# Summing the squares of a norm on TensorE quarter by quarter instead of adding them on VectorE first

## The chip, the cores and the metric

One core of a Trainium2 chip. TensorE (PE) multiplies matrices into eight PSUM banks, VectorE (DVE) and ScalarE (ACT) work element by element, SyncE (SP) issues the loads; the engines run their own instruction streams and meet at semaphores. The metric is the device time of one execution of the whole program, in microseconds: the median of several runs.

## The reference

Two transformer blocks over 256 positions and 1024 channels in float32, one after the other. The first has two layers, each of a token mixer (attention, latent attention, two convolution branches) and a feed-forward part. What matters here is the norm with which each part begins, and the residual ahead of it:

```python
def rmsnorm(x, g):
    xf = x.astype(jnp.float32)
    y = xf * lax.rsqrt(jnp.mean(xf * xf, axis=-1, keepdims=True) + NORM_EPS)
    return (y * g.astype(jnp.float32)).astype(x.dtype)
...
def channel_mixing(x, shift, scale, g_pre, w_up, ffn_conv, w_down, g_post):
    h = rmsnorm(x, g_pre) * (1.0 + scale) + shift
    a, b = jnp.split(h @ w_up, 2, axis=-1)
    y = (jax.nn.silu(causal_dwconv(a, ffn_conv)) * b) @ w_down
    return rmsnorm(y, g_post)
```

and in the block `x = x + gate * token_mixing(...)`, then `x = x + gate * channel_mixing(...)`.

## The kernel before

The activations lie transposed: 1024 channels are 8 chunks of 128 partitions, each with the 256 positions as columns, so `x` is 128 x 2048 and a *quarter* is two chunks (128 x 512). The program is a list of stages: m0, f0, m1, f1 of the first block (m a mixer, f a feed-forward part), then 16 stages of the second. Weights come in tiles of 128 x 1024 through a ring of 11 landing places. Every float32 product is made of three: ScalarE casts a weight tile to a high part (`whi`, L460), VectorE subtracts to get the low part (`wlo`, L472), activations are split the same way, and `mm3` (L512 to L514) adds high x high, high x low and low x high. A tile can't be used before its `w_lo` signal. ScalarE and VectorE split a few tiles ahead of TensorE, at places that are written out in their programs.

A stage of the first block that isn't m0 begins before its norm is known ("early" stages: f0, m1, f1). `early_scalar` and `early_vector` scale and add the last stage's output into `x` quarter by quarter (L886, L888), and make `u`, which is `x` times the channel gains, without the norm's factor, which is the same for all channels of a position (high part L826, low part L896). `early_tensor` (L576) multiplies three pairs of weight tiles by `u`: its `step` 0 to 9 takes one chunk of `u` each, 6 groups of 3 matmuls while all three projections are in it, 12 matmuls in steps 0 and 1 and 6 in each of steps 8 and 9, as the third projection lags by two steps. Meanwhile ScalarE squares each quarter (L824, L830: `square`, 0 to 3). To sum over channels, which lie on partitions, TensorE multiplies by a matrix of ones in plain float32 (L601); that gives the sum in all 128 partitions of bank 7 (`MISC`). Before the change VectorE first adds the four quarters of squares into one (`squares_vector`, L867, three adds, called in `early_vector` between quarters 2 and 3 of `u`), and TensorE then sums the two chunks left after step 4 (`SUMS_AFTER`), and signals `sumsq`.

From `sumsq` on: ScalarE takes a logarithm and an exponential (L681, L683), VectorE the variance (L858) and Newton steps (L689 to L693), then for each of the eight chunks the normed value (L926), ScalarE its high part `h` (L847) and VectorE the low part (L931). The results of the early projections are read from their banks with the norm's factor (`lead_vector`, L614 and L615; `lead_scalar`, L623), between splits of the next tiles. In an f stage the next projections (j = 3, 4, 5, each a pair of tiles, multiplied by `h`) follow, then down-projection 0, j = 6 and 7, down-projection 1, and so on. Each j is drawn through taps (L1150, L1154), silu (L1122) and a product `up_read` (L1164), which frees the bank, and `inner` (L1127, L1168), which the down-projection reads. j = 7 uses the bank of j = 4. In m1 there follow the fourth `cf` projection (L1507, L1754), and projections `scu`, `qk` with convolution taps on VectorE (L1769).

Engines take their instructions strictly in this written order, waiting at each semaphore.

Of the kernel before, what the change touches and what calls it, by code (L numbers as in the profile page):

```python
# [11 lines left out]
ALU = mybir.AluOpType  # L12
# [4 lines left out]
T = 256  # L17
# [267 lines left out]
def lead_operand(g):  # L285
    return Lead(g.ra1[:, 2528:6656].rearrange("p (a n) -> p a n", a=2))


def bc2(ap):
    return ap.unsqueeze(1).broadcast_to([ap.shape[0], 2, ap.shape[1]])  # L290


def v2(ap):
    return ap.rearrange("p (a t) -> p a t", a=2)


def xk(t, k):
    return t[:, k * T:(k + 1) * T]
# [165 lines left out]
def split_vector(g, dve, upto):  # L464
    D_, W = g.m.done, g.m.when
    while g.ahead["dve"] < min(upto, len(g.split)):
        i = g.ahead["dve"]
        n = g.split[i]
        g.ahead["dve"] = i + 1
        w = g.weights(n)  # L470
        dve.wait_ge(*W("w_hi", n))
        dve.tensor_tensor(w.lo, g.slot(n), w.hi.bitcast(F32), ALU.subtract).then_inc(*D_("w_lo", n))  # L472
        modulation_vector(g, dve, n)
# [30 lines left out]
def take_tensor(g, pe, name, i):  # L504
    g.skip("pe")
    n = g.next("pe", name, i)
    pe.wait_ge(*g.m.when("w_lo", n))
    return n


def mm3(pe, out, w, x, first, last, skip=False):
    pe.matmul(out, w.hi, x.hi, start=first, stop=False, skip_group_check=skip)  # L512
    pe.matmul(out, w.hi, x.lo, start=False, stop=False, skip_group_check=skip)  # L513
    return pe.matmul(out, w.lo, x.hi, start=False, stop=last, skip_group_check=skip)  # L514
# [10 lines left out]
def halves(j):  # L525
    return 2 * j, 2 * j + 1
# [26 lines left out]


EARLY_STAGES = ("f0", "m1", "f1")
LEAD, LAG, SUMS_AFTER = 3, 2, 4
LEAD_ORDER = ((1, 0), (2, 0), (0, 0), (0, 1), (1, 1), (2, 1))


# [11 lines left out]
def lead_banks(st, j):  # L571

    return (j, 4 + j) if st[0] == "m" else (4 + j, j)


def early_tensor(g, pe, st, projections):  # L576


    D_, W = g.m.done, g.m.when
    u, parts, sums = lead_operand(g), [], g.ps[MISC]  # L580
    pe.wait_ge(*W("u_shift", st))
    for step in range(8 + LAG):
        if step < 8:
            pe.wait_ge(*W("u", st, step))
        for j, (name, at) in enumerate(projections):
            k = step - LAG * (j == LEAD - 1)
            for i, half in enumerate(halves(at)):
                bank = lead_banks(st, j)[i]
                if k == 0:
                    pe.wait_ge(*W(*g.banks.use(bank, "lead_read", st, 2 * j + i)))  # L590
                    parts.append(take_tensor(g, pe, name, half))
                if 0 <= k < 8:
                    mm = mm3(pe, g.ps[bank][:, 0:WIDE], g.weights(parts[2 * j + i])[:, k * 128:(k + 1) * 128], u.chunk(k),
                             k == 0, k == 7, skip=True)
                    if k == 7:
                        mm.then_inc(*D_("tile", parts[2 * j + i]))
        if step == SUMS_AFTER:
            pe.wait_ge(*W(*g.banks.use(MISC, "newton", st, 0)))
            pe.wait_ge(*W("squares", st, 3))
            for c in range(2):  # L600
                mm = pe.matmul(sums[:, 0:T], g.C("ones", 0, 128), xk(squares_buffer(g, st), c), start=c == 0, stop=c == 1)  # L601
            mm.then_inc(*D_("sumsq", st))


def lead_out(g, i):
# [38 lines left out]
MISC = 7  # L644
# [71 lines left out]
def quarter(p):  # L716
    return slice(p * 512, (p + 1) * 512)
# [48 lines left out]
def squares_buffer(g, st):  # L766
    return g.fa1[:, 2048:4096] if st in FIRST else g.fa2[:, 13056:15104]
# [90 lines left out]
    dve.tensor_scalar(g.small[:, 0:T], g.ps[MISC][:, 0:T], 1.0 / D, 1e-6, ALU.mult, ALU.add).then_inc(*D_("var", st))  # L858


def squares_vector(g, dve, st, p):
    D_, W = g.m.done, g.m.when
    sq = squares_buffer(g, st)
    dve.wait_ge(*W("square", st, p))
    if p > 1:
        dve.wait_ge(*W("squares", st, p - 1))
    dve.tensor_tensor(sq[:, quarter(0)], sq[:, quarter(0)], sq[:, quarter(p)], ALU.add).then_inc(*D_("squares", st, p))  # L867


def early_vector(g, dve, st, shift, A):  # L870

    D_, W = g.m.done, g.m.when
    u, prev = lead_operand(g), BEFORE[st]
    v, r = g.small[:, 0:T], g.small[:, T:2 * T]
    ysquare_vector(g, dve, prev)
    dve.wait_ge(*W("u_shift_hi", st))
    dve.tensor_tensor(u.shifts()[1], g.mod[:, shift:shift + 8].unsqueeze(2).broadcast_to([128, 8, 2]),
                      u.shifts()[0].bitcast(F32), ALU.subtract).then_inc(*D_("u_shift", st))
    split_vector(g, dve, g.ahead["dve"] + 1)
    normed_vector(g, dve, prev)  # L880
    dve.wait_ge(*W("gain", st))
    for p in range(5):
        if p < 4:
            t, s = g.t(p), g.x[:, quarter(p)]
            dve.wait_ge(*W("y_gated", prev, p))
            dve.tensor_tensor(v2(t), v2(t), bc2(r), ALU.mult).then_inc(*D_("y_scaled", prev, p))  # L886
            dve.wait_ge(*W("y_scaled", prev, p))
            dve.tensor_tensor(s, s, t, ALU.add).then_inc(*D_("x", st, p))  # L888
        if p == 4:
            squares_vector(g, dve, st, 1)  # L890
            squares_vector(g, dve, st, 2)
            squares_vector(g, dve, st, 3)
        for k in halves(p - 1) if p else ():
            c = u.chunk(k)
            dve.wait_ge(*W("u_hi", st, k))
            dve.scalar_tensor_tensor(c.lo[:, 0:T], xk(g.x, k), A[:, k:k + 1], c.hi[:, 0:T].bitcast(F32), ALU.mult,  # L896
                                     ALU.subtract).then_inc(*D_("u", st, k))
        if p == 1:
            split_vector(g, dve, g.ahead["dve"] + 1)
    split_vector(g, dve, g.ahead["dve"] + 2)  # L900


def modulated_vector(g, dve, st, gname, lay, shift, scale):
# [11 lines left out]
    if st != "m0":  # L915
        early_vector(g, dve, st, a - scale + shift, A)
        var_vector(g, dve, st)
# [53 lines left out]
def ysquare_vector(g, dve, st):  # L971

    D_, W = g.m.done, g.m.when
    sq = g.fa1[:, 2048:4096]
    for p in (1, 2):
        dve.wait_ge(*W("ysquare", st, p))
        if p == 2:
            dve.wait_ge(*W("ysquares", st, 1))
        dve.tensor_tensor(sq[:, quarter(0)], sq[:, quarter(0)], sq[:, quarter(p)], ALU.add).then_inc(*D_("ysquares", st, p))
# [36 lines left out]
def normed_vector(g, dve, st):  # L1016
    D_, W = g.m.done, g.m.when
    v, r = g.small[:, 0:T], g.small[:, T:2 * T]
    dve.wait_ge(*W("var_ln", "y", st))
    dve.tensor_scalar(v, g.ps[MISC][:, 0:T], 1.0 / D, 1e-6, ALU.mult, ALU.add).then_inc(*D_("var", "y", st))  # L1020
    rsqrt_vector(g, dve, ("y", st), r, v, g.t(8)[:, 0:T], g.t(8)[:, T:2 * T])
    dve.wait_ge(*W("factor", "y", st))
# [70 lines left out]
def ffn_tensor(g, pe, st, up, up0, down, dn0, R):  # L1093
    early_tensor(g, pe, st, [(up, up0 + j) for j in range(LEAD)])
    for p in range(NF // 2):
        for j in halves(p):
            if j >= LEAD:
                proj_tensor(g, pe, up, up0 + j, up_bank(j), ("up_read", st, j), g.h, chunks("h", st) if j == LEAD else None)
        for q in downs_behind(p):
            down_tensor(g, pe, st, down, dn0 + q, q, R[q % 3])  # L1100
# [182 lines left out]
def mix_tensor(g, pe, st, lay):  # L1283
# [5 lines left out]
    for step, i, bank in mix_banks(lay):  # L1289
        ps = g.ps[bank] if bank is not None else None  # L1290
        if (step, i, bank) == lead[0] and lay:
            early_tensor(g, pe, st, [mix_projection(st, lay, *s)[:2] for s in lead])
        elif (step, i, bank) == lead[0]:
            lead_tensor(g, pe, [mix_projection(st, lay, *s) for s in lead], g.h, chunks("h", st))
# [2535 lines left out]
```

## Time and profile before

| | us |
|---|---|
| median of 3 runs | 3313.85 |
| the runs | 3311.53 to 3317.24 |
| the profiled execution: time | 3317.55 |
| the profiled execution: span | 3315.8 |
| PE busy | 3170.8 (96%) |
| DVE busy | 2488.2 (75%) |
| ACT busy | 1779.0 (54%) |

The span runs from the first to the last instruction; the time has a little more around it. Rows of the trace give an instruction's start, its duration, engine, line, output and inputs, and in brackets how long the engine was idle before it and who ended the wait. Matmuls overlap: a row of 0.28 us begins 0.12 us after the one before. PEclk is TensorE's granted clock as a share of full speed.

### The profile page before, as it was taken

What the parts mean: (1) busy time and instruction counts of PE and PEld (TensorE: products, weight loads), DVE (VectorE), ACT (ScalarE), POOL (GpSimd) and SP (SyncE); (2) the same over time, 40 slices, a digit from 0 to 9 for tenths busy, and PEclk for the clock granted to TensorE, in tenths of its full rate; (3) what the DMA queues carried; (4) which work ended last, traced back from release to release, by engine and by line L of the source; (5) the groups of instructions that cost most, each with busy time, mean ns of one, the idle gap of its engine ahead of it and who ended that gap; (6) DMA issues with size and microseconds to landing.
All of it is one profiled execution on the core that took longest, in us unless ns stands there. A gap on an engine that the chain in (4) does not pass through costs nothing.

```text
span 3315.8 us, 64468 instructions
## 1 busy us (share of the span) xinstructions
PE 3170.8 (96%) x27118; PEld 3082.9 (93%) x27118; DVE 2488.2 (75%) x3822; ACT 1779.0 (54%) x2723; POOL 3.0 (0%) x6
## 2 busy tenths in 40 slices
PE   6899999989999999989999999999999999998999
PEld 6889999888999999879999989999979999987999
DVE  8888799987887766787676667667667667678766
ACT  4556554555564545665454546455456455456544
POOL 0000000000000000000000000000000000000000
PEclk8999999999999999999999999999999999999999
DMA  7456478444746555435555544555544555543453
GB/s 288 130 178 225 167 277 321 145 126 138 244 173 230 169 189 187 157 99 188 190 184 187 189 134 169 187 182 191 188 137 149 187 184 189 188 165 103 162 190 129
DMA packets 164353, 597.94 MB, mean 180 GB/s; under 512 B 18240, under 2 KB 18272, under 8 KB 163936
## 3 DMA queue, kind: packets, MB, share of 16 engines
q1 hardware_dynamic: 164064, 593.81, 53.3%
q8 instruction: 215, 3.52, 0.4%
q14 instruction: 74, 0.61, 0.1%
HBM read 592.69 MB, written 1.05 MB: 179 GB/s over the span
## 4 chain that ended last, share of the span: by engine, by line
PE 74%; DVE 16%; ACT 6%; issue 2%; DMA 1%; SPq 0%; DVEq 0%; ACTq 0%
PE ps L512 24%; PE ps L513 24%; PE ps L514 24%; DVE wlo L472 4%; ACT whi L460 2%; DVE fa L1769 1%; DVE land L658 1%; DVE fa L2663 0%; DMA land<-w_ada 0%; DMA land<-w_in 0%; DVE tmps L691 0%; DVE h L2017 0%; DVE tmps L689 0%; PE ps L2515 0%; DVE tmps L2372 0%
## 5 line engine op out<-in xcount | busy, mean ns | idle before, releaser
L512 PE MATMUL ps<-h,whi 128*128 128x256 f32 x5280 | 1489.9, 282 | 34.9 <-DVE h L931 13.9
L514 PE MATMUL ps<-h,wlo 128*128 128x256 f32 x5328 | 1491.6, 280 | 0.0
L513 PE MATMUL ps<-h,whi 128*128 128x256 f32 x5280 | 1478.5, 280 | 0.0
L472 DVE TENSOR_TENSOR wlo<-land,whi 128x1024 fp32r<-128x1024 f32 (+1 forms) x1026 | 1210.4, 1217 | 252.1 <-ACT whi L460 250.7
L460 ACT ACTIVATE whi<-land 128x1024 fp32r<-128x1024 f32 (+1 forms) x1026 | 1023.8, 1045 | 155.5 <-PE ps L514 129.2
L512 PEld LDWEIGHTS ps<-h,whi 128*128 128x128 f32 x5280 | 997.1, 189 | 44.0 <-issue 27.2
L514 PEld LDWEIGHTS ps<-h,wlo 128*128 128x128 f32 x5328 | 1005.7, 189 | 0.0
L513 PEld LDWEIGHTS ps<-h,whi 128*128 128x128 f32 x5280 | 997.3, 189 | 0.8
L513 PE MATMUL ps<-y,whi 128*128 128x256 f32 x1472 | 410.9, 279 | 0.0
L512 PE MATMUL ps<-y,whi 128*128 128x256 f32 x1472 | 410.9, 279 | 0.0
L514 PE MATMUL ps<-y,wlo 128*128 128x256 f32 x1472 | 410.9, 279 | 0.0
L2214 ACT ACTIVATE tmps<-tmps 128x256 f32<-128x256 f32 x176 | 74.1, 421 | 487.2 <-DVE tmps L2245 487.2
L512 PE MATMUL ps<-ra,whi 128*128 128x256 f32 (+2 forms) x1088 | 314.2, 289 | 10.3 <-DVE ra L1674 5.8
L513 PE MATMUL ps<-ra,whi 128*128 128x256 f32 (+2 forms) x1088 | 308.0, 283 | 0.0
L514 PE MATMUL ps<-ra,wlo 128*128 128x256 f32 (+2 forms) x1088 | 307.3, 282 | 0.0
L512 PEld LDWEIGHTS ps<-y,whi 128*128 128x128 f32 x1472 | 276.6, 188 | 0.0
L514 PEld LDWEIGHTS ps<-y,wlo 128*128 128x128 f32 x1472 | 276.6, 188 | 0.0
L513 PEld LDWEIGHTS ps<-y,whi 128*128 128x128 f32 x1472 | 276.6, 188 | 0.0
L512 PEld LDWEIGHTS ps<-ra,whi 128*128 128x128 f32 (+1 forms) x1088 | 207.1, 190 | 14.9 <-issue 8.5
L513 PEld LDWEIGHTS ps<-ra,whi 128*128 128x128 f32 (+1 forms) x1088 | 207.1, 190 | 0.6
L2245 DVE TENSOR_TENSOR tmps<-ps,small 128x512 f32<-128x512 f32 x176 | 121.5, 690 | 114.6 <-PE ps L514 114.4
L514 PEld LDWEIGHTS ps<-ra,wlo 128*128 128x128 f32 (+1 forms) x1088 | 207.0, 190 | 0.0
(470 smaller groups left out, 2904.1 us busy)
## 6 DMA issues: line engine op xcount, KB each, us to landing
land<-w_gu SPq DMA_DIRECT2D x352, 512.0 KB, 3.6
land<-w_dn SPq DMA_DIRECT2D x176, 512.0 KB, 3.5
land<-w_in SPq DMA_DIRECT2D x136, 512.0 KB, 3.5
land<-w_ada SPq DMA_DIRECT2D x96, 512.0 KB, 4.4
land<-w_up SPq DMA_DIRECT2D x88, 512.0 KB, 3.8
land<-hg_in SPq DMA_DIRECT2D x64, 512.0 KB, 3.5
land<-w_down SPq DMA_DIRECT2D x44, 512.0 KB, 4.1
land<-ple_gate SPq DMA_DIRECT2D x32, 512.0 KB, 3.5
```

Source lines behind the costliest of these rows:

```text
L460: act.activation(w.hi, g.slot(n), ACT.Copy).then_inc(*D_("w_hi", n))
L472: dve.tensor_tensor(w.lo, g.slot(n), w.hi.bitcast(F32), ALU.subtract).then_inc(*D_("w_lo", n))
L512: pe.matmul(out, w.hi, x.hi, start=first, stop=False, skip_group_check=skip)
L513: pe.matmul(out, w.hi, x.lo, start=False, stop=False, skip_group_check=skip)
L514: return pe.matmul(out, w.lo, x.hi, start=False, stop=last, skip_group_check=skip)
L658: dve.scalar_tensor_tensor(w, w, 1.0, g.crow[:, :], ALU.mult, ALU.mult, accum_out=g.mod[:, i:i + 1]).then_inc(*D_("ada", i))
L1769: dve.scalar_tensor_tensor(o, M.cu[:, j, n:n + 256], g.P("cf_conv", lay * 124 + 4 * n + j), o, ALU.mult, ALU.add).then_inc(*D_("conv", st, ...
L2214: act.activation(b[:, 0:T], a[:, 0:T], ACT.Silu).then_inc(*D_("silu", st, j))
L2245: dve.tensor_tensor(v2(a), v2(g.ps[4 + j % 3][:, :]), bc2(r), ALU.mult).then_inc(*D_("up_read", st, j))
```

## The change

The constant `SUMS_AFTER` becomes a tuple of four steps. After step 2 TensorE waits for the bank and for the squares of quarter 0 and multiplies the two chunks of that quarter by the ones; after steps 4, 5 and 6 it does the same for quarters 1, 2 and 3, all accumulating into the same bank; `sumsq` is signalled with the last. VectorE's three adds and the function that made them are gone. It holds for f0, m1 and f1.

```diff
-LEAD, LAG, SUMS_AFTER = 3, 2, 4
+LEAD, LAG, SUMS_AFTER = 3, 2, (2, 4, 5, 6)
...
-        if step == SUMS_AFTER:
-            pe.wait_ge(*W(*g.banks.use(MISC, "newton", st, 0)))
-            pe.wait_ge(*W("squares", st, 3))
-            for c in range(2):
-                mm = pe.matmul(sums[:, 0:T], g.C("ones", 0, 128), xk(squares_buffer(g, st), c), start=c == 0, stop=c == 1)
-            mm.then_inc(*D_("sumsq", st))
+        if step in SUMS_AFTER:
+            p = SUMS_AFTER.index(step)
+            if p == 0:
+                pe.wait_ge(*W(*g.banks.use(MISC, "newton", st, 0)))
+            pe.wait_ge(*W("square", st, p))
+            for k in halves(p):
+                mm = pe.matmul(sums[:, 0:T], g.C("ones", 0, 128), xk(squares_buffer(g, st), k), start=k == 0, stop=k == 7)
+            if p == 3:
+                mm.then_inc(*D_("sumsq", st))
...
-def squares_vector(g, dve, st, p):
-    D_, W = g.m.done, g.m.when
-    sq = squares_buffer(g, st)
-    dve.wait_ge(*W("square", st, p))
-    if p > 1:
-        dve.wait_ge(*W("squares", st, p - 1))
-    dve.tensor_tensor(sq[:, quarter(0)], sq[:, quarter(0)], sq[:, quarter(p)], ALU.add).then_inc(*D_("squares", st, p))
...
-        if p == 4:
-            squares_vector(g, dve, st, 1)
-            squares_vector(g, dve, st, 2)
-            squares_vector(g, dve, st, 3)
```

## Rows read from the trace of the kernel before

**Rows 1.** The page: busy time by engine, and shares of the last chain.
```profile
PE 3170.8 (96%) x27118; PEld 3082.9 (93%) x27118; DVE 2488.2 (75%) x3822; ACT 1779.0 (54%) x2723; POOL 3.0 (0%) x6
...
PE 74%; DVE 16%; ACT 6%; issue 2%; DMA 1%; SPq 0%; DVEq 0%; ACTq 0%
```

**Rows 2.** Line L601: count, duration in ns (min/median/max), first and last start.
```profile
L601 PE MATMUL ps<-fa,con x12: 377/378/379, 404.7 to 961.8; 128*128 128x256 f32 x12
```

**Rows 3.** Timeline of PE in f0: start, duration (us), line, output and inputs.
```profile
404.62 0.28 PE L514 MATMUL ps<-ra,wlo 128*128 128x258 f32 x1
404.73 1.02 PE L601 MATMUL ps<-fa,con 128*128 128x256 f32 x4
...
405.71 0.28 PE L513 MATMUL ps<-ra,whi 128*128 128x258 f32 x1
...
413.50 0.28 PE L512 MATMUL ps<-h,fr 128*128 128x256 f32 x1
...
430.36 0.28 PE L512 MATMUL ps<-ra,whi 128*128 128x256 f32 x1
...
441.56 0.28 PE L512 MATMUL ps<-h,whi 128*128 128x256 f32 x1
```

**Rows 4.** Timeline of DVE in f0.
```profile
400.55 2.27 DVE L867 TENSOR_TENSOR fa<-fa 128x512 f32<-128x512 f32 x3
402.74 0.88 DVE L896 SCALAR_TENSOR_TENSOR ra<-x,small,ra 128x256 fp32r<-128x256 f32 x2
...
406.30 0.42 DVE L858 TENSOR_SCALAR small<-ps 128x256 f32<-128x256 f32 x1 [0.42 <-ACT tmps L681]
...
409.20 0.48 DVE L931 SCALAR_TENSOR_TENSOR h<-fa,mod,h 128x256 fp32r<-128x256 f32 x1 [0.18 <-ACT h L847]
...
414.62 0.48 DVE L931 SCALAR_TENSOR_TENSOR h<-fa,mod,h 128x256 fp32r<-128x256 f32 x1 [0.18 <-ACT h L847]
...
415.57 2.36 DVE L472 TENSOR_TENSOR wlo<-land,whi 128x1024 fp32r<-128x1024 f32 x2
...
429.13 0.43 DVE L1168 TENSOR_TENSOR ra<-tmps,ra 128x256 fp32r<-128x256 f32 x1 [0.49 <-ACT ra L1127]
...
440.65 0.41 DVE L1164 TENSOR_TENSOR tmps<-fa,ps 128x256 f32<-128x256 f32 x1
```

**Rows 5.** Timeline of ACT in f0.
```profile
399.86 0.63 ACT L824 ACTIVATE fa<-x 128x512 f32<-128x512 f32 x1 [0.69 <-DVE x L888]
...
405.80 0.48 ACT L681 ACTIVATE tmps<-ps,con 128x256 f32<-128x256 f32 x1 [2.59 <-PE ps L601]
...
414.50 3.89 ACT L460 ACTIVATE whi<-land 128x1024 fp32r<-128x1024 f32 x4
```

**Rows 6.** Timelines of DVE and PE in m1.
```profile
620.35 0.76 DVE L1754 SCALAR_TENSOR_TENSOR fa<-tmps,fa 128x256 f32<-128x256 f32 x2 [2.25 <-ACT tmps L1507]
...
629.95 2.35 DVE L472 TENSOR_TENSOR wlo<-land,whi 128x1024 fp32r<-128x1024 f32 x2
...
631.22 0.58 PE L512 MATMUL ps<-h,whi 128*128 128x256 f32 x1 [4.44 <-DVE wlo L472]
```

**Rows 7.** Timelines of DVE and PE in f1, at projection j=7.
```profile
998.25 0.41 DVE L1164 TENSOR_TENSOR tmps<-fa,ps 128x256 f32<-128x256 f32 x1
...
998.81 0.36 PE L512 MATMUL ps<-h,whi 128*128 128x256 f32 x1 [0.64 <-DVE tmps L1164]
```

**Rows 8.** Windows: stretch, length, busy PE PEld DVE ACT POOL, PEclk, DMA share, GB/s.
```profile
685.40:697.60 12.20, 5.91 (x30) 3.82 (x30) 10.44 (x33) 7.67 (x21) 0.00 (x0) 0.71 0.14 44
918.70:932.00 13.30, 11.14 (x94) 11.17 (x95) 10.95 (x17) 7.04 (x11) 0.00 (x0) 1.00 0.43 146
631.20:635.90 4.70, 4.68 (x22) 4.68 (x23) 4.70 (x11) 0.00 (x0) 0.00 (x0) 0.50 0.00 0
697.60:704.20 6.60, 6.34 (x23) 5.32 (x24) 5.49 (x20) 3.58 (x16) 0.00 (x0) 0.50 0.01 4
2455.20:2458.70 3.50, 3.37 (x16) 2.53 (x16) 0.00 (x0) 1.68 (x4) 0.00 (x0) 0.51 0.00 0
```

## The prediction

> **What bounds the kernel now.** I read the page first: TensorE is busy for 96% of the span and holds 74% of the chain that ended last, VectorE 16% [rows 1]. These are averages over 20 stages. The change touches three places only, the norms at the start of f0, m1 and f1, so I went there: the timelines of PE, DVE and ACT, one engine at a time, over the start of f0 (395 to 455 us), m1 (590 to 690) and f1 (950 to 1010), looking for who arrives last at each hand-over.
>
> In f0 TensorE works off `early_tensor` without a hole: steps 5 to 9 are 66 matmuls, and from the second of them at 405.71 to the first matmul on `h` at 413.50 there are 65 intervals, 0.120 us each [rows 3]. The sums at 404.73 wait for nobody: the three VectorE adds began at 400.55 and were over before 402.8 (2.27 us together), 1.9 us before TensorE came to them [rows 3, 4]. From the sums hangs a second chain: ScalarE stood idle for 2.59 us until they were done at 405.80 [rows 5], then VectorE takes the variance at 406.30, the Newton steps, eight chunks of `h` (the first done at 409.68, the last at 415.10) and the split of the next weight tile at 415.57 [rows 4]. So in `early_tensor` two chains run side by side: TensorE's own stream, and sums, factor, `h`, splits, taps on ScalarE and VectorE. The question for every edit is which of the two it lengthens, and how much the second has in hand.
>
> Its slack is small. In f0 TensorE reaches down-projection 0 at 430.36 while its last operand is done at 429.56 (0.80 us in hand), and projection j=7 at 441.56 while `up_read` of j=4, which frees its bank, ends at 441.06 (0.50 in hand) [rows 3, 4]. In f1 the same place is already late: TensorE idles 0.64 us for L1164 (998.25 + 0.41 = 998.66, resumed 0.15 later: I take 0.15 as the hand-over) [rows 7]. In m1 TensorE idles 4.44 us until 631.22 for the split that starts at 629.95, and the VectorE chain before it had waited last, 2.25 us until 620.35, for a ScalarE tanh which itself reads what the chain delivers [rows 6]. So in m1 and f1 the second chain sets the time, and in f0 it nearly does.
>
> **Removed: nine VectorE adds.** `squares_vector` runs three times in each stage; the three adds of f0 are one row, which holds 402.74 - 400.55 = 2.19 us of VectorE's stream [rows 4]; m1 and f1 have the same. What stands behind them is the low part of chunks 6 and 7 (L896, 402.74), which TensorE needs at step 6, after 407, and two splits; then VectorE waits for the variance, which needs the sums. All of it comes 2.19 us earlier and ends in a longer wait. Worth: 0.
>
> **Added: six f32 matmuls a stage.** The 12 records of L601 in three stages are two for each of the two matmuls [rows 2]. From the matmul at 404.62 to the second one behind the sums at 405.71 are 1.09 us, where two plain intervals would be 0.24: the pair costs 0.85 us [rows 3]. After the change there are four pairs instead of one: 3 x 0.85 = 2.55 us a stage on TensorE, 7.7 in all. That is a measured price of the same matmul in the same place; an end below it would need TensorE to have been waiting there, and it was not.
>
> **Moved: the last pair.** Before, all is summed after step 4. Now the pairs stand after steps 2, 4, 5 and 6, and `sumsq`, on which the whole second chain waits, is only signalled by the last. Ahead of it TensorE now has three more pairs (2.55) and steps 5 and 6 (2 x 18 matmuls x 0.120 = 4.31): 6.86 us later. The squares are no reason for it: ScalarE's last square starts at 399.86 and takes 0.63 [rows 5], long before step 5. The waits on `square` therefore cost nothing; behind each on PE's queue stand only the following steps.
>
> **What the later sums do, f0.** Everything of the second chain moves by 6.86, since it had waited for the sums (ACT idle 2.59). TensorE's own stream ends 2.55 later, at 416.05. (a) The first `h` comes at 409.68 + 6.86 + 0.15 = 416.7, 0.6 us idle; the last at 422.1, so projection j=3 ends about 422.8; three projections take 430.36 - 413.50 = 16.9, one 5.6, so the stream alone would end it at 421.7. (b) j=4 needs its split: ScalarE casts four tiles only after `h` (L460 at 414.50) [rows 5], VectorE's first split ends near 416.75, so 423.8: 0.9 idle. (c) j=4 and j=5 are 11.2 us, to 435.0; down-projection 0 needs the operand of 429.56, now 436.57: 1.6 idle, 6.21 behind before. (d) j=7 would start at 447.8 and gets its bank at 441.06 + 6.86 + 0.15 = 448.1: 6.5 behind. After that the trace shows TensorE without holes to the end of f0, so nothing absorbs it. The idle pieces are not further terms; together with the 2.55 they make up the 6.5.
>
> **m1.** The wait at 631.22 ends with a VectorE split of the second chain: 6.86 later. TensorE's 2.55 vanish in its wait, which grows from 4.44 to about 8.8 us. **f1.** The wait at 998.81 likewise: 6.86. Sum: 6.5 + 6.86 + 6.86 = 20.2 us. The profiled execution has a span of 3315.8 and a time of 3317.55, so 3336.0 and 3337.8 for it; it lies 3.7 above the median of the runs shown, 3313.85. I put the sum on the median: 3334.1.
>
> **The unknown: the clock.** The longer hole in m1 may change what the clock does. At the hole of 4.44 the granted clock was 0.50 of full speed from 631.20 to 635.90, 4.7 us that did 2.35 us of full-speed work. After other holes the half-speed stretch (1.2 GHz for 2.4) lasted from 3.5 us (0.51 from 2455.20) to 6.6 us (0.50 from 697.60 to 704.20) [rows 8]. So m1 may turn out 0.6 better or 1.0 worse than the sum; I take no change. In f0 and f1 new holes of 0.3 to 1.6 us appear where there were none or 0.64. Nearest rows: in the 13.3 us from 918.70, of which TensorE idled 2.16 in one hole at the start, the clock stayed 1.00; in the 12.2 us from 685.40 it was busy for 5.91 only, in pieces, and the clock fell to a mean of 0.71 [rows 8]. I take "stays"; the other end is up to 3.3 us in either stage (half of 6.6), part of which the 1.6 us hole would hide.
>
> The skill speaks against the change in two places. The Trainium skill, Perfetto Trace Analysis, section Matmul Optimizations, says that the matmul engine scales its power with utilisation, so matmuls should run back to back in batches; holes in three more batches would by that rule give the last rival below, and the trace so far bears it out only for long or clustered holes. Its section Identifying the Most-Contended Engine tells to optimise the engine with the highest occupancy first; this change puts work on it. Counted by that engine's work alone the sum would be that of the first rival, 7.7 us.
>
> **Rivals.**
> (1) *Only TensorE's own work counts*, the later chain being hidden: 3 x 2.55 = 7.7, 3321.5. For it: TensorE is the 96% engine. Against: the waits at 631.22 and 998.81, and 0.50 us of slack in f0. Chance 0.07.
> (2) *VectorE's relief comes through, faster.* If TensorE reached the sums before the adds were done, taking them away would bring `sumsq`, `h` and the splits forward by up to 2.19 a stage, and in m1 and f1 VectorE does pace TensorE. Price -3 x 2.19 = -6.6: 3307.3. It decides only if step 4 ends before about 402.8; it ends at 404.73, and the last pair moves later on top of that. Chance 0.03.
> (3) *Mostly hidden, no measurable change.* The change does not do what it says, or later parts absorb it: for instance ScalarE or VectorE regain the delay within the idle time that they have at other points of m1, down to 5 us or less. Against: the waits named are ends of this very chain. Chance 0.04, about 3317.
> (4) *The clock falls in f0 and f1 too*, and stays down longer in m1: 2 x 2 to 3.3, + 1: 3339 to 3342. Chance 0.13.
> The forecast has the remaining 0.73, with a range of its own from 3331 to 3337 (0.6 to 1.0 of the clock, 0.3 a stage on the hand-overs, some 1.5 of run to run spread).
>
> **Range.** 3326 to 3341: it takes in the forecast, most of (4) and the half-hidden cases between (1) and it, and leaves out (2), (3) and (1). What a measurement of this kernel can tell from no change is about 0.2%, 6.6 us. Faster by more than that 0.03, within it 0.04, slower 0.93.
>
> **What would show it.** L601 with 48 records instead of 12, L867 gone; PE's step 2 to step 9 longer by 2.55 us in each stage, with the last pair some 6.9 us later counted from the first matmul of the stage; ACT's idle time ahead of L681 about 9.5 us instead of 2.59; VectorE idle some 9 us before L858. In m1 the wait ahead of the split grows to 8 or 9 us, in f1 the wait at j=7 gives way to several (for `h`, for a split, for down-projection 0), in f0 the same ones appear. If the L601 rows come where I say but down-projection 0 in f0 is under 4 us late, the slack was misread; if m1 is right and f0 and f1 are off by 2 or more each, it is the clock; if the extra pairs cost other than 0.85, the price of interleaved f32 matmuls is wrong.

## The result: 0.66% slower, and the profile after

| | before | after |
|---|---|---|
| median, us | 3314.55 (4 runs) | 3337.11 (4 runs, 3336.49 to 3337.27) |
| ratio | | 1.0066, 95% interval 1.0054 to 1.0078 |
| profiled execution: time, span | 3317.55, 3315.8 | 3336.49, 3334.7 |
| f0, m1, f1 in the profiled execution | 195.77, 360.68, 189.24 | 202.65, 368.22, 194.93 |

A stage is measured here and below from its first matmul on `u` (the first of 258 columns) to that of the next such stage, and f1 to the first matmul on the squares of its output. The changed kernel is slower by 22.6 us on the medians and by 18.9 in the two profiled spans; 3334.1 had been forecast, 20.2 more. By stage the profiled pair gives +6.88, +7.54 and +5.69 where 6.5, 6.86 and 6.86 had been worked out. Behind f1, where both kernels have the same instructions, the changed one was 1.1 us shorter in this pair.

The page after, its busy times and the line of the sums (count, duration in ns, first and last start), answers [rows 1, 2]:

```profile
PE 3179.9 (95%) x27154; PEld 3090.4 (93%) x27154; DVE 2482.8 (74%) x3813; ACT 1776.0 (53%) x2723; POOL 3.0 (0%) x6
...
L603 PE MATMUL ps<-fa,con x48: 377/378/382, 400.3 to 983.1; 128*128 128x256 f32 x48
```

VectorE has nine instructions fewer and TensorE 36 more, and TensorE's share fell although it has more to do: what grew is its waiting. The timeline of PE in f0 after, answering [rows 3]:

```profile
400.33 1.03 PE L603 MATMUL ps<-fa,con 128*128 128x256 f32 x4
...
405.50 1.02 PE L603 MATMUL ps<-fa,con 128*128 128x256 f32 x4
...
408.51 1.03 PE L603 MATMUL ps<-fa,con 128*128 128x256 f32 x4
...
416.75 0.36 PE L512 MATMUL ps<-h,fr 128*128 128x256 f32 x1 [0.59 <-DVE h L921]
...
423.66 0.38 PE L512 MATMUL ps<-h,whi 128*128 128x256 f32 x1 [0.67 <-DVE wlo L472]
...
436.63 0.35 PE L512 MATMUL ps<-ra,whi 128*128 128x256 f32 x1 [1.51 <-DVE ra L1158]
...
448.00 0.36 PE L512 MATMUL ps<-h,whi 128*128 128x256 f32 x1
```

The four pairs are there (the fourth starts at 411.54), none waits for its squares, and behind them stand the holes in the order of the working: for the first `h`, for a split, for the operand of down-projection 0. The other two engines in f0 after, answering [rows 4, 5]:

```profile
402.18 2.36 DVE L472 TENSOR_TENSOR wlo<-land,fr 128x1024 fp32r<-128x1024 f32 x2 [0.47 <-ACT fr L460]
413.11 0.42 DVE L861 TENSOR_SCALAR small<-ps 128x256 f32<-128x256 f32 x1 [8.57 <-ACT tmps L684]
...
435.92 0.43 DVE L1158 TENSOR_TENSOR ra<-tmps,ra 128x256 fp32r<-128x256 f32 x1 [0.48 <-ACT ra L1117]
```
```profile
412.60 0.48 ACT L684 ACTIVATE tmps<-ps,con 128x256 f32<-128x256 f32 x1 [9.51 <-PE ps L603]
```

Before, the same splits were

```profile
403.53 2.35 DVE L472 TENSOR_TENSOR wlo<-land,fr 128x1024 fp32r<-128x1024 f32 x2
```

So VectorE reaches them 1.35 us earlier, not 2.19, as it now waits for ScalarE's casts (0.47 us here), and then it idles 8.57 us instead of 0.42 for the norm's factor. The freed time went into waits, whole. The operand of down-projection 0 ends at 436.35 where it was 429.56, with the stage starting 0.10 sooner: 6.9 us later. In m1 and f1 after, answering [rows 6, 7]:

```profile
644.91 0.58 PE L512 MATMUL ps<-h,whi 128*128 128x256 f32 x1 [7.13 <-DVE wlo L472]
...
1007.48 0.36 PE L512 MATMUL ps<-ra,whi 128*128 128x256 f32 x1 [1.48 <-DVE ra L1158]
...
1020.02 0.36 PE L512 MATMUL ps<-h,whi 128*128 128x256 f32 x1 [1.10 <-DVE tmps L1154]
```

In m1 the one long wait grew from 4.44 to 7.13 us. The stage had begun at 590.72 before and at 597.50 after, so the matmul behind that wait comes 644.91 - 631.22 - 6.78 = 6.91 us later within its stage. In f1 the matmul of j=7 comes 1020.02 - 998.81 - (965.73 - 951.40) = 6.88 later.

### The profile page after: what moved, and what is told of

It is laid out like the page before. It is cut to its first block, busy times and chain, and to the rows that moved or that the text cites. A ratio compares the mean times of both kernels' runs of the same rounds, so it can differ in the third digit from the quotient of the medians.

```text
span 3334.7 us, 64525 instructions
## 1 busy us (share of the span) xinstructions
PE 3179.9 (95%) x27154; PEld 3090.4 (93%) x27154; DVE 2482.8 (74%) x3813; ACT 1776.0 (53%) x2723; POOL 3.0 (0%) x6
## 4 chain that ended last, share of the span: by engine, by line
PE 74%; DVE 17%; ACT 6%; issue 3%; DMA 1%; SPq 0%; ACTq 0%; DVEq 0%
PE ps L512 24%; PE ps L513 24%; PE ps L514 24%; DVE wlo L472 4%; ACT whi L460 2%; DVE fa L1759 1%; DVE land L661 1%; DVE fa L2653 0%; DMA land<-w_ada 0%; DMA land<-w_in 0%; DVE tmps L694 0%; DVE tmps L692 0%; DVE h L2007 0%; PE ps L603 0%; DVE attn L2653 0%
## 5 line engine op out<-in xcount | busy, mean ns | idle before, releaser
L512 PE MATMUL ps<-h,whi 128*128 128x256 f32 x5280 | 1491.2, 282 | 38.7 <-DVE h L921 13.2
```

## The experiments

Stage lengths from the profiled execution of each kernel, in us, and the time against the kernel before, run on the same chip:

| kernel | f0 | m1 | f1 | ratio, 95% interval |
|---|---|---|---|---|
| before | 195.77 | 360.68 | 189.24 | |
| before, again | 195.61 | 361.51 | 188.05 | one run |
| changed | 202.65 | 368.22 | 194.93 | 1.0066 (1.0054 to 1.0078) |
| changed, again | 202.24 | 368.23 | 194.93 | one run |
| pe_load | 198.29 | 361.45 | 189.75 | 1.0017 (1.0008 to 1.0027) |
| late_signal | 199.51 | 364.72 | 193.35 | 1.0039 (1.0025 to 1.0053) |
| early_quarters | 197.73 | 363.35 | 191.28 | 1.0021 (1.0012 to 1.0031) |
| adds_kept | 202.83 | 367.71 | 195.92 | 1.0069 (1.0054 to 1.0084) |
| hole_filled | 202.37 | 367.30 | 194.90 | 1.0059 (1.0042 to 1.0076) |
| m1_only_early | 195.60 | 358.23 | 189.21 | 0.9999 (0.999 to 1.0008) |

Matmuls came in two paces at the same granted clock, which has to be known to read this table. The windows from 1040 to 1120 of five executions (before, before again, changed, changed again, adds_kept), all in f1 and dense, PE alone (busy time, matmuls, PEclk, DMA share, GB/s):

```profile
1040.00:1120.00 80.00, 80.00 (x682) 1.00 0.63 214
```
```profile
1040.00:1120.00 80.00, 80.00 (x688) 1.00 0.63 217
```
```profile
1040.00:1120.00 80.00, 80.00 (x687) 1.00 0.66 226
```
```profile
1040.00:1120.00 80.00, 80.00 (x688) 1.00 0.65 228
```
```profile
1040.00:1120.00 80.00, 80.00 (x682) 1.00 0.66 225
```

682 or 687 to 688 matmuls in the same 80 us. The kernel before had either (189.24 and 188.05 us of f1), so the pace is of the execution and not of the change. Shorter stretches of the slow pace stand in f0 and m1 as well. late_signal, early_quarters and m1_only_early have the slow one (0.1177 us a matmul), pe_load and hole_filled the fast one (0.1167). Like with like, the change costs f1 194.93 - 188.05 = 6.88 at the fast pace, and 195.92 - 189.24 = 6.68 at the slow one (with adds_kept).

**TensorE's added work without the later signal.** The kernel before with

```diff
             mm.then_inc(*D_("sumsq", st))
+        if step in (5, 6, 7):
+            if step == 5:
+                pe.wait_ge(*W("y_gated", BEFORE[st], 3))
+            for c in range(2):
+                pe.matmul(g.ps[3][:, 0:T], g.C("ones", 0, 128), xk(squares_buffer(g, st), c), start=c == 0, stop=c == 1)
```

> The kernel before (VectorE adds, one pair of sums after step 4), and three more pairs of the same f32 matmuls on TensorE after steps 5, 6 and 7, into a bank that nothing reads (they compute nothing that is used): TensorE's added work alone, with the signal of the sums where it was. Theory of two chains: TensorE's stream is 2.55 us longer a stage; that counts in f0 in full, vanishes in m1 in the 4.44 us wait, and counts less the wait of 0.64 in f1: 2.55 + 0 + 1.9 = 4.5 us over before. Rival, only TensorE's work counts: 7.7 us. If the matmuls are the whole cause of the 22 us: about 22.

Measured: 3321.64 against 3315.79, 5.9 us; by stage +2.5 in f0, -0.1 in m1 against the second trace of before (both have a half-speed stretch at 920 us, see below), +1.7 in f1 at the same pace. Expected were 2.55, 0 and 1.9; the stages add up to 4.2 us against 4.5. The interval of the time is 2.7 to 9.0 us, which leaves out 22 but not the 7.7 of the first rival; what speaks against that one is m1, which didn't grow. TensorE's work counts where it is the bound, and m1 swallows it. These pairs stand behind the signal of the sums. The same count of f32 matmuls as in the changed kernel, a quarter of its loss.

**The later signal without added work.**

```diff
-LEAD, LAG, SUMS_AFTER = 3, 2, 4
+LEAD, LAG, SUMS_AFTER = 3, 2, 6
```

> The kernel before with its single pair of sums after step 6 instead of step 4, nothing else: the signal comes two steps later (4.31 us), TensorE's work is the same. Two chains: 4.31 in m1 and f1, 3.8 in f0, where 0.5 is in hand: 12.4 us over before. Rival, only TensorE's work counts: 0.

Measured: 3328.98 against 3315.79, 13.2 us; by stage +3.74, +4.04, +4.11. Not one instruction was added. ScalarE's wait for the sums in f0, [rows 5] before, is now

```profile
409.98 0.48 ACT L681 ACTIVATE tmps<-ps,con 128x256 f32<-128x256 f32 x1 [6.94 <-PE ps L601]
```

2.59 + 4.35. The position of one pair of matmuls in TensorE's stream costs more than three pairs behind the signal do.

**All four pairs, as early as the single one.** The changed kernel with

```diff
-LEAD, LAG, SUMS_AFTER = 3, 2, (2, 4, 5, 6)
+LEAD, LAG, SUMS_AFTER = 3, 2, (1, 2, 3, 4)
```

> The changed kernel with its four pairs after steps 1, 2, 3 and 4 instead of 2, 4, 5 and 6: as much work on TensorE as in the changed kernel, but the last pair where the single one stood before. Two chains: the signal is late by the three added pairs less the 0.3 us that TensorE idles ahead of step 2, 2.3 us, and each stage by about as much: 7 us over before, 15 under the changed kernel. Rival, the price is that of breaking the stream with more f32 pairs wherever they stand: no change against the changed kernel, 22 over before.

Measured: 3323.24 against 3315.79, 7.5 us; by stage +1.96, +2.67, +2.04 (f0, m1, f1; f1 at the slow pace of the first trace of before). ScalarE's wait for the sums in f0:

```profile
409.15 0.48 ACT L684 ACTIVATE tmps<-ps,con 128x256 f32<-128x256 f32 x1 [4.85 <-PE ps L603]
```

4.85 where before had 2.59: 2.26 more for the three pairs. The same instructions as in the changed kernel, two thirds of its loss gone by their place alone. What is left is the price of three pairs ahead of the signal, which hold it back: m1, which swallowed the pairs of pe_load, pays for these.

**VectorE's relief.** The changed kernel with three additions a stage put back as dead work:

```diff
+        if p == 4:
+            for n in range(1, 4):
+                dve.wait_ge(*W("square", st, n))
+                sq = squares_buffer(g, st)
+                dve.tensor_tensor(g.t(4 + n), sq[:, quarter(0)], sq[:, quarter(n)], ALU.add).then_inc(*D_("squares", st, n))
         for k in halves(p - 1) if p else ():
```

> The changed kernel with three VectorE additions a stage put back as dead work (same operands sizes, same place in VectorE's program, results unused). Theory: VectorE's 2.19 us a stage were hidden behind the wait for the sums, so no difference from the changed kernel (within 1 us). Rival, the relief of VectorE gave something back: up to 6.6 us over the changed kernel.

Measured: 3338.48, 1.0069 over before, where the changed kernel has 1.0066: no difference. By stage +0.2, -0.5, +1.0 against the changed kernel, the last by the pace of f1. VectorE in f0 with them:

```profile
400.60 1.89 DVE L887 TENSOR_TENSOR tmps<-fa 128x512 f32<-128x512 f32 x3
402.40 0.87 DVE L891 SCALAR_TENSOR_TENSOR ra<-x,small,ra 128x256 fp32r<-128x256 f32 x2
...
413.27 0.42 DVE L861 TENSOR_SCALAR small<-ps 128x256 f32<-128x256 f32 x1 [7.72 <-ACT tmps L684]
```

They took 402.40 - 400.60 = 1.80 us, somewhat less than the original three, which waited for each other, and the wait behind them is 7.72 instead of 8.57 us. The two times can't decide this, as their intervals together are some 6 us wide either way, as much as the rival's 6.6. The trace can: counted from the start of the stage, the wait for the operand of down-projection 0 ends at 41.74 us in f0 (41.78 in the changed kernel), the long wait of m1 at 47.40 (47.41), and the wait at j=7 of f1 at 54.28 (54.30). The rival wanted up to 2.19 there. The +0.2 in f0 comes behind that point, with the slow pace.

The -0.5 in m1 is another matter. 0.34 us of it arise at one place far behind the norm, in VectorE's stream, the changed kernel first and then this one:

```profile
793.70 0.69 DVE L696 SCALAR_TENSOR_TENSOR tmps<-tmps 128x512 f32<-128x512 f32 x1
794.85 0.75 DVE L1863 SCALAR_TENSOR_TENSOR fa<-fa,small,tmps 128x512 f32<-128x512 f32 x1 [0.46 <-DVE tmps L696]
```
```profile
794.04 0.69 DVE L696 SCALAR_TENSOR_TENSOR tmps<-tmps 128x512 f32<-128x512 f32 x1
794.85 0.75 DVE L1868 SCALAR_TENSOR_TENSOR fa<-fa,small,tmps 128x512 f32<-128x512 f32 x1
```

From one start to the next are 1.15 us in the first and 0.81 in the second, and TensorE waits for what follows (4.20 us against 3.85). The pause stands in all four traces of kernels that have no VectorE adds in any stage (changed, changed again, early_quarters, hole_filled) and in none of the other six. Why is open.

**The clock in m1.** In the changed kernel the granted clock is at half speed through most of the hole and 5.5 us beyond it, then full; the windows of the changed kernel (columns as in [rows 8]):

```profile
638.08:645.21 7.13, 0.30 (x1) 0.30 (x2) 7.10 (x18) 4.65 (x6) 0.00 (x0) 0.65 0.21 75
645.21:650.70 5.49, 5.49 (x28) 5.49 (x28) 5.49 (x14) 0.00 (x0) 0.00 (x0) 0.52 0.00 0
650.70:656.00 5.30, 5.30 (x48) 5.30 (x47) 5.30 (x6) 2.49 (x3) 0.00 (x0) 1.00 0.56 198
```

28 matmuls in 5.49 us against 48 in 5.30. Is that on the path? The changed kernel with the hole filled:

```diff
         elif step == "qk":
+            if lay and i == 1:
+                warm_tensor(g, pe, 14)
```

> The changed kernel with 14 f32 matmuls of constants (6.0 us, into a bank that nothing reads) ahead of projection qk 1 in m1, in the hole of 7.13 us after which the clock stood at half speed for 10.2 us. If the clock is on the path there, m1 gets 2.6 us shorter (half of the 5.2 us that it ran at half speed after work resumed). If VectorE and ScalarE pace m1 there in any case (as in the run with three extra pairs, where the clock did not fall and a hole of 1.49 us appeared behind the first), m1 gets shorter by 0.7 us at most, and new waits for them appear between qk 1 and the token-major projection.

Measured: 3333.95, 1.0059 over before; m1 is 367.30, 0.9 us shorter. PE in m1, from this kernel:

```profile
644.18 0.39 PE L512 MATMUL ps<-h,whi 128*128 128x256 f32 x1 [1.09 <-DVE wlo L472]
...
651.54 0.39 PE L512 MATMUL ps<-h,whi 128*128 128x256 f32 x1 [1.43 <-DVE wlo L472]
```
```profile
640.00:652.00 12.00, 9.48 (x67) 1.00 0.21 67
```

The clock stays full and TensorE, faster now, runs into a new wait of 1.43 us for the next split, so that is what sets the time there. TensorE's next wait that both kernels have ends 72.97 us into m1 in the changed kernel and 72.21 here. So of the 2.6 us that half speed took from its work, 0.76 were on the path, and the rest was hidden behind VectorE's splits. My bound of 0.7 was a little low. The other 0.15 of the 0.9 arise behind the last hole of the stage, far from the filled one. The times of the two kernels (1.0059 and 1.0066) can't tell the difference.

**A version that turns the finding round.** If the signal is what counts, give it sooner where TensorE has time: the kernel before, with quarter-by-quarter sums in m1 alone.

```diff
+        if st == "m1":
+            for p in {1: (0, 1), 2: (2, 3)}.get(step, ()):
+                if p == 0:
+                    pe.wait_ge(*W(*g.banks.use(MISC, "newton", st, 0)))
+                pe.wait_ge(*W("square", st, p))
+                for k in halves(p):
+                    mm = pe.matmul(sums[:, 0:T], g.C("ones", 0, 128), xk(squares_buffer(g, st), k), start=k == 0, stop=k == 7)
+                if p == 3:
+                    mm.then_inc(*D_("sumsq", st))
+        elif step == SUMS_AFTER:
...
-        if p == 4:
+        if p == 4 and st != "m1":
```

> The kernel before, with the sums quarter by quarter in m1 alone, two pairs after step 1 and two after step 2, none added on VectorE there. Two chains: the signal comes two steps sooner (4.31), with three pairs more (2.55) less the 0.3 that TensorE idles ahead of step 2, so 2.1 us earlier; of this ScalarE, busy with two casts until about 403.2 on f0's clock, takes 1.9. TensorE's 2.3 us more vanish in its wait of 4.44. So m1 shorter by 1.9, f0 and f1 unchanged: 1.9 under before, less than times can show; the trace shows it by stage. Rival, TensorE's work counts everywhere: m1 longer by 2.3.

Measured: 3314.25 against 3314.71, ratio 0.9999 (0.999 to 1.0008): by time, no change. By stage m1 is 358.23, 2.4 us shorter than the first trace of before and 3.3 shorter than the second, f0 and f1 as they were. The first is the one to compare with, since the second had a half-speed stretch late in m1 that this trace hasn't. ScalarE and TensorE in m1, from this kernel:

```profile
598.96 0.48 ACT L690 ACTIVATE tmps<-ps,con 128x256 f32<-128x256 f32 x1 [0.54 <-PE ps L603]
```
```profile
628.93 0.38 PE L512 MATMUL ps<-h,whi 128*128 128x256 f32 x1 [0.44 <-DVE wlo L472]
...
636.29 0.39 PE L512 MATMUL ps<-h,whi 128*128 128x256 f32 x1 [1.50 <-DVE wlo L472]
```

ScalarE waits 0.54 us for the sums instead of 2.59, the hole of 4.44 is down to 0.44, and the clock does not fall behind it. Counted from the start of the stage, that wait ends 1.74 us sooner than in the first trace of before, where I had expected 1.9; at TensorE's next wait (of 0.37 us in both) it is 2.12, the 0.38 between goes with the half speed that the kernel before had there; the last 0.3 comes in small pieces over the rest of the stage. It is the direction in which this edit is worth something, in one stage of three; it is no proven gain in time.

**The two kernels once more.**

> The kernel before once more, for a second trace: f1 took 189.24 us in the first, at 0.1178 us a matmul, where the changed kernel had 0.1168 in f1. If this pace differs from execution to execution, this trace can have either; if the change made it faster, it has 0.1178 again.

> The changed kernel once more: the same question, 0.1168 again or 0.1178. With 0.1178 its f1 would be 196 us instead of 194.93.

The kernel before had the fast pace in f1 this time (188.05), the changed one again the fast pace and to the hundredth the same f1 (194.93). Spans 3312.3 and 3334.3, 22.0 apart: +6.63, +6.72, +6.88 in the three stages, 1.8 in the rest. m1 of before was 0.8 us longer than in its first trace. Up to its last hole (330 us into the stage) it was 0.6 shorter; behind it, at half speed, 1.4 longer. The windows of before and of before again, PE alone:

```profile
920.00:924.00 4.00, 3.14 (x26) 1.00 0.31 112
```
```profile
920.00:924.00 4.00, 4.00 (x22) 0.57 0.09 35
```

## Why the prediction was right, point by point

**What bounds.** Two chains from the start of the stage, TensorE's stream and the one behind `sumsq`: shown by pe_load and late_signal, which lengthen one each. In f0 the first costs 2.5 and the second 3.7, in f1 1.7 and 4.1, in m1 nothing and 4.0. The two don't add up to the change, in m1 least of all (4.0 of 7.5), because the three pairs of the changed kernel stand ahead of the signal and delay it. The experiment for that part is early_quarters, with 2.0, 2.7 and 2.0; together with late_signal it gives 5.7, 6.7 and 6.2. Had only TensorE's work counted (rival 1), late_signal would have cost nothing.

**Removed, worth 0.** Right for the chain behind the norm: adds_kept. "All of it comes 2.19 us earlier" was not right: the splits came 1.35 earlier, held by ScalarE's casts. And the kernels without the adds have 0.34 us more in m1, by VectorE's pause shown above, which nothing in the prediction foresaw.

**Added, 0.85 us a pair.** Right. From the second pair at 405.50 to the third at 408.51 are 3.01 us after the change, one pair and one step (0.85 + 2.16).

**Moved, 6.86 us.** Right: ScalarE's wait for the sums went from 2.59 to 9.51, 6.92 more, and in late_signal by 4.35 for the two steps alone, where I had 4.31.

**f0, 6.5.** The two traces of each kernel give 6.88 and 6.63. The holes stood where they had been put: 0.59 for the first `h` (0.6 forecast), 0.67 for the split (0.9), 1.51 for down-projection 0 (1.6), and j=7 started at 448.00 where 448.1 was worked out. At j=7 the changed kernel is 448.00 - 441.56 + 0.10 = 6.54 us behind, which is the forecast; the rest of the 6.88 comes in the dense part behind it, where the slow pace lasted longer. Windows of f0 in the changed kernel, first and second trace, PE alone:

```profile
440.00:520.00 80.00, 80.00 (x680) 1.00 0.80 286
```
```profile
440.00:520.00 80.00, 79.99 (x684) 1.00 0.80 290
```

Four matmuls are 0.47 us, and f0 is 0.41 shorter in the second.

**m1, 6.86.** The place is right (6.91 at the wait that was named), but the stage is 7.54 us longer, so the term was 0.7 too small. (Against the second trace of before it is 6.72, but that one has the late half-speed stretch of 1.4 us, which neither trace of the changed kernel has.) The size of the new wait was wrong, 7.13 and not 8.8. I had taken 4.44 + 6.86 - 2.55, as if TensorE lost nothing else ahead of it, but it waits 0.28 for the first `h` and 0.68 for a split there, as in f0, and for later chunks of `h` in pieces too short for a row. These holes take from the large one and leave its end where it was. Behind the wait two things come on top of the 6.91. The half-speed stretch, open in the prediction, lasted 5.5 us instead of 4.7. It put 0.76 us on the path in the changed kernel (hole_filled) and, by the comparison with m1_only_early, 0.38 before, so the change costs 0.4 by it: TensorE's next wait ends 7.29 us later than before. VectorE's pause of 0.34 is the other. What is left is 0.1 the other way, in small pieces.

**f1, 6.86.** 5.69 in the profiled pair, 6.88 at equal pace. The difference of 1.2 us is not the change's: at j=7, ahead of the dense part, the profiled pair has the 6.88 as well.

**The clock in f0 and f1** (rival 4) stayed full in spite of the new holes, as the nearest row had it. The Trainium skill (Perfetto Trace Analysis, section Matmul Optimizations) says that the matmul engine scales its power with utilisation, so matmuls should run back to back in batches. The traces agree in m1, where the granted clock was 0.52 over the 5.49 us behind the hole of 7.13; the new holes of 0.59 to 1.51 us in f0 and f1 left it at 1.00 (over 404 to 450 and 985 to 1022). The Trainium skill (Perfetto Trace Analysis, section Identifying the Most-Contended Engine) says to optimise the engine with the highest occupancy first. For an edit that adds to that engine's work this has the right sign, and the work alone, by this case's rows 3 x 2.55 = 7.7 us, is a third of the size: the larger part of the loss came from a signal that this engine gives late, which its occupancy doesn't show.

**The sum.** 20.2 against 22.6 on medians, 18.9 and 22.0 in pairs of spans. The measured 3337.11 lies 0.1 above the forecast's own range of 3331 to 3337 and inside 3326 to 3341: 2.4 us above 3334.1 by the difference, and 0.7 because the median of before is 3314.55 with its fourth run. Of the 2.4, the term of m1 was 0.7 too small; the rest is less than the program behind f1 varies by. Its instructions are the same in all ten traces, and it took from 2172.4 to 2176.7 us. With the two traces of the kernel before 3.5 us apart in their spans, a sum as near as this is partly luck; the mechanism rests on the stages.

## What to carry to other kernels

Where an engine's stream carries a signal that another chain waits for, ask first where in the stream the signal stands, then what the instructions cost. Here three pairs of matmuls behind the signal cost 1.7 to 2.5 us in the two stages where they counted at all and nothing in the third, ahead of it 2.0 to 2.7 in every stage, and the pair that signals, moved by two steps, cost 3.7 to 4.1. Work taken from an engine that then waited for the same signal was worth nothing, however busy that engine is over the whole program; look for the wait in front of its next dependent instruction. Compare traces by stage, with a second trace of the same kernel beside them, before a microsecond is given a cause.

## What the runs showed of the hardware that was not expected

The same matmul stream in f1, dense and at a granted clock of 1.00, ran at 0.1167 us a matmul in some executions and at 0.1177 in others (688 against 682 in 80 us), in the same kernel, and stretches of both stand in the other stages. What sets it stays open; it was not tried.

The hole of 2.2 us late in m1 was followed by a clock of 1.00 in one execution of the kernel before and by half speed (0.57 over the next 4 us) in another, which lost 1.4 us by it. Of all ten traces only that one and pe_load have it.

A VectorE instruction late in m1 started 1.15 us behind the one ahead of it instead of 0.81 in every kernel whose VectorE adds in the norms were gone from all stages. The cause is open.
